# State-space rows kept by lag instead of by time step, and two groups of full-width matmuls cut into pieces of 32 stationary columns

## What is computed

```
u = h @ w_in                                # (256, 1024), 64 groups of 16 channels
per group, 64 complex states:
    bu = u_group @ bb^T                     # injection into the states
    h_t = a * h_(t-1) + bu_t                # scan over time
    y = Re(h @ c^T) + d * u                 # emission and skip
y = gelu(y); val, gate = split(y @ w_glu); out = val * sigmoid(gate)
```

## Time and profile before

| what | value |
|---|---|
| time, median of 3 runs | 767.78 us (765.35 to 768.37) |
| the profiled execution: its own time | 767.76 us |
| its span, first to last instruction | 765.8 us |
| TensorE busy (matmul records) | 727.7 us, 95% of the span |
| VectorE (DVE) | 530.4 us, 69% |
| ScalarE (ACT) | 411.9 us, 54% |
| GpSimd (POOL) | 127.7 us, 17% |
| mean granted TensorE clock | 0.984 |

### The profile page before, as it was taken

How to read it: one execution, slowest core, us unless ns; L and a number is a source line. 1 busy time by engine, 2 the same in 40 slices (tenths; PEclk the granted TensorE clock), 3 DMA queues, 4 the chain that set the end, 5 groups by cost and what they waited for, 6 DMA issues and landing times.

```text
span 765.8 us, 17216 instructions
## 1 busy us (share of the span) xinstructions
PE 727.7 (95%) x6636; PEld 660.5 (86%) x6636; DVE 530.4 (69%) x897; ACT 411.9 (54%) x682; POOL 127.7 (17%) x120
## 2 busy tenths in 40 slices
PE   4789999999999999999999999989999999999996
PEld 1478999457888999999999799979969999999995
DVE  4756665995488788777867686556567767676665
ACT  4244644565465556675567653325556555555554
POOL 1000000211015343434303254430000000000000
PEclk9799999999999999999999999989999999999998
DMA  8979755696755767667676041008725555555521
GB/s 315 378 272 383 255 190 165 255 406 246 283 215 182 280 187 257 209 238 238 221 260 204 3 138 58 29 29 342 263 73 192 177 183 174 192 191 165 192 83 56
DMA packets 46068, 156.61 MB, mean 205 GB/s; under 512 B 6016, under 2 KB 7312, under 8 KB 46016
## 3 DMA queue, kind: packets, MB, share of 16 engines
q1 hardware_dynamic: 43344, 148.26, 55.2%
q10 hardware_dynamic: 2160, 6.38, 2.2%
q0 software_dynamic: 512, 1.25, 0.4%
HBM read 154.82 MB, written 1.05 MB: 204 GB/s over the span
## 4 chain that ended last, share of the span: by engine, by line
PE 85%; DVE 7%; issue 3%; ACT 3%; POOL 1%; DMA 1%; DVEq 0%; POOLq 0%; ACTq 0%
PE up L368 13%; PE up L370 13%; PE up L369 13%; PE acc L368 9%; PE acc L369 9%; PE acc L370 9%; PE gv L410 5%; DVE wlo L1165 2%; PE misc L469 1%; PE up L752 1%; DVE tmp L1193 1%; PE up L765 1%; PE acc L740 1%; DMA ident<-in_ident 1%; PE acc L498 1%
## 5 line engine op out<-in xcount | busy, mean ns | idle before, releaser
L1165 DVE TENSOR_TENSOR wlo<-raw,whi 128x1024 fp32r<-128x1024 f32 x188 | 252.7, 1358 | 77.2 <-ACT whi L820 70.8
L368 PE MATMUL up<-hh,whi 128*128 128x256 f32 x896 | 255.7, 285 | 1.9 <-DVE hl L1198 1.9
L370 PE MATMUL up<-hh,wlo 128*128 128x256 f32 x896 | 253.5, 283 | 0.0
L369 PE MATMUL up<-hl,whi 128*128 128x256 f32 x896 | 253.5, 283 | 0.0
L820 ACT ACTIVATE whi<-raw 128x1024 fp32r<-128x1024 f32 x185 | 192.5, 1051 | 41.0 <-PE acc L370 26.3
L368 PEld LDWEIGHTS up<-hh,whi 128*128 128x128 f32 x896 | 171.7, 192 | 9.8 <-issue 3.8
L369 PEld LDWEIGHTS up<-hl,whi 128*128 128x128 f32 x896 | 171.8, 192 | 0.0
L370 PEld LDWEIGHTS up<-hh,wlo 128*128 128x128 f32 x896 | 171.8, 192 | 0.0
L1496 DVE SCALAR_TENSOR_TENSOR ffn<-up,conv,ffn 128x254 f32<-128x254 f32 (+1 forms) x176 | 72.7, 475 | 45.6 <-ACT ffn L1015 45.3
L368 PE MATMUL acc<-ah,whi 128*128 128x256 f32 x352 | 99.8, 284 | 0.6 <-DVE wlo L1165 0.6
L369 PE MATMUL acc<-al,whi 128*128 128x256 f32 x352 | 99.6, 283 | 0.0
(11 more groups left out here) (240 smaller groups left out, 920.6 us busy)
## 6 DMA issues: line engine op xcount, KB each, us to landing
raw<-in_w SPq DMA_DIRECT2D x188, 512.0 KB, 3.4
mraw<-in_mw SPq DMA_DIRECT2D x48, 512.0 KB, 6.1
arena<-in_mw SPq DMA_DIRECT2D x24, 512.0 KB, 9.7
raw<-in_w SPq DMA_DIRECT2D x12, 256.0 KB, 13.0
tmp<-in_mw SPq DMA_DIRECT2D x6, 512.0 KB, 7.7
ffn<-in_mw SPq DMA_DIRECT2D x6, 512.0 KB, 8.5
tmp<-in_mw ACTq DMA_DIRECT2D x4, 512.0 KB, 6.0
ffn<-in_mw ACTq DMA_DIRECT2D x4, 512.0 KB, 8.6
```

Of the source, the lines that this page charges most:

```text
L368: pe.matmul(out, w_h, xh, start=first, stop=False, skip_group_check=skip)
L369: pe.matmul(out, w_h, xl, start=False, stop=False, skip_group_check=skip)
L370: return pe.matmul(out, w_l, xh, start=False, stop=last, skip_group_check=skip)
L1165: dve.tensor_tensor(wlo[:, n % SPL, :], raw[:, n % RAW, :], whi[:, n % SPL, :].bitcast(F32), ALU.subtract).then_inc(lo_ready, 1)
```

## The change

It touches the state-space mixer and `spread_root`:

- `u` and `up` are kept with the lag outside: column l·64 + j instead of 4·j + l. The reads of `stack_u` and `lags` and the writes of `lags` and `emit` become contiguous. ACT's copy of the projection reads PSUM 4 columns apart, and ACT's gelu reads its input 64 columns apart to bring `yg` back into the order of time.
- `inject` and `spread_root` issue each matmul as four, of 32 stationary columns and 32 output partitions each, with the same moving columns.

```
-        u = ffn[:].rearrange("p (m j l) -> p m j l", m=KT, l=LCH)
+        u = ffn[:].rearrange("p (m l j) -> p m l j", m=KT, l=LCH)
...
                 for h in range(2):
-                    mm = pe.matmul(spread[:, h * P:(h + 1) * P], rt[:, h:h + 1].broadcast_to([P, P]), ident[:],
-                                   start=True, stop=True)
+                    for g in range(0, P, 32):
+                        mm = pe.matmul(spread[g:g + 32, h * P:(h + 1) * P], rt[:, h:h + 1].broadcast_to([P, 32]), ident[:],
+                                       start=True, stop=True)
...
-                                       ident[:, 32 * q:32 * q + 32], u[:, mt, :, l], start=True, stop=True)
+                                       ident[:, 32 * q:32 * q + 32], u[:, mt, l, :], start=True, stop=True)
...
-                        mm = pe.matmul(acc[:, 2 + mt % 2, (2 * q + r) * NJ:(2 * q + r + 1) * NJ],
-                                       bpow_r[:, r, c:c + P], ust[:, mt % 2, q, :], start=True, stop=True)
+                        for g in range(0, P, 32):
+                            mm = pe.matmul(acc[g:g + 32, 2 + mt % 2, (2 * q + r) * NJ:(2 * q + r + 1) * NJ],
+                                           bpow_r[:, r, c + g:c + g + 32], ust[:, mt % 2, q, :], start=True, stop=True)
...
-                y = up[:, mt % 2, 0:T].rearrange("p (j l) -> p j l", l=LCH)
+                y = up[:, mt % 2, 0:T].rearrange("p (l j) -> p l j", l=LCH)
                 for lag in range(LCH):
-                    pe.matmul(y[:, :, lag:LCH], kbd[:, mt, lag, :], u[:, mt, :, 0:LCH - lag],
+                    pe.matmul(y[:, lag:LCH, :], kbd[:, mt, lag, :], u[:, mt, 0:LCH - lag, :],
...
-                            mm = pe.matmul(y[32 * q:32 * q + 32, :, l], cpow[:, (l + 1) % 4, r, pair * 32:pair * 32 + 32],
+                            mm = pe.matmul(y[32 * q:32 * q + 32, l, :], cpow[:, (l + 1) % 4, r, pair * 32:pair * 32 + 32],
...
-                act.activation(yg[:, mt, :], yv[:, mt % 2, :], ACT.Gelu_apprx_tanh).then_inc(yg_ready, 1)
+                act.activation(yg[:, mt, :].rearrange("p (j l) -> p j l", l=LCH), yv[:, mt % 2, :].rearrange("p (l j) -> p j l", l=LCH),
+                               ACT.Gelu_apprx_tanh).then_inc(yg_ready, 1)
...
-                act.activation(ffn[:, m * T:(m + 1) * T], acc[:, m % 2, 0:T], ACT.Copy).then_inc(u_ready, 1)
+                act.activation(u[:, m, :, :], acc[:, m % 2, 0:T].rearrange("p (j l) -> p l j", l=LCH), ACT.Copy).then_inc(u_ready, 1)
```

## The result

| what | before | after |
|---|---|---|
| median of the compared runs | 766.64 us (764.66 to 768.37, 11 runs) | 762.22 us (761.55 to 765.09, 11 runs) |
| ratio | | 0.9949, interval 0.9935 to 0.9963 |
| profiled execution: own time, span | 767.76, 765.8 | 762.10, 760.1 |
| mean granted TensorE clock | 0.984 | 0.986 |

The ratio puts the change at the very edge of the 0.5% that counts. A second set of runs of the same kernel, 0.9962 (0.9949 to 0.9975), lies inside it. So: a gain of 0.4 to 0.5%, some 3 to 4 us.

What follows compares the result with a forecast made beforehand. TensorE was taken as the bound in the state-space stage's middle, at 8.90 us an iteration. Stage terms -4.09 + 0.75 + 0.6 + 1.1 = -1.64, with -0.35 for the root, gave -1.99 from 767.76: 765.8 us, range 762.3 to 768.3.

Steps and rivals of the forecast that it cites:

- The stack: TensorE's stack in the state-space stage: contiguous moving columns bring it to the emission's pace, -0.41 us each.
- The injection: TensorE's injection in the state-space stage: 64 pieces at the emission's pace plus switches of form, -0.51 us each.
- Lags and emission: TensorE's lags and emission groups in the state-space stage: no gain from the new column order.
- ACT: ACT's two copies in the state-space stage, now reading with a stride: no change from 0.383 us.
- Emission 0: First emission of the state-space stage: a DVE split goes ahead and delays POOL's chain, +0.75 us, between 0 and +1.1.
- The middle: Full stretch of the state-space iterations: one stall from DVE and POOL blocking each other, +0.6 us, between 0 and 1.9.
- Iteration 7: Last iteration of the state-space stage: five DVE operations meet POOL's last two, +1.1 us, between 0 and 1.5.
- The root: The root's spread at five norms: an earlier first weight load, together -0.35 us, between 0 and -0.8.
- (a): Rival for the whole kernel: TensorE alone decides, DVE and POOL blocks fall into slack, 763.3 us; chance 0.25.
- (b): Rival in the state-space stage: DVE and POOL become the bound, iterations settle at 8.36, total 767.1 us; chance 0.13.
- (c): Rival in the injection: pieces sharing moving columns don't overlap, +2.3 us on each, total 779 us; chance 0.06.
- (d): Rival in the emission: contiguous PSUM writing saves up to half of its 0.92 us, total 763.5 us; chance 0.04.

Runs made afterwards that it cites:

- a2_whole: The changed kernel run once more, unedited: ratio 0.9962 to the kernel before, state-space stage 73.97 us.
- e9_short_split: The changed kernel with DVE's weight splits of iterations 2 to 6 cut to 32 of 1024 columns: ratio 0.9958 to the kernel before, stage 71.17 us.
- e10_fill: The changed kernel with stack ahead of emission, skip 5 ahead of a split, and more GLU products ahead of emission 7: ratio 0.9899 to before, median 758.17 us.
- e12_gelu_plain: The changed kernel with the gelu reading and writing straight on, rows not returned to time order: stage 73.59 us, one execution of 763.50 us.
- e8_both: The changed kernel with the stack ahead of the emission and skip 5 ahead of a DVE split: ratio 0.9925 to the kernel before, median 760.82 us.
- e7_stack_first: The changed kernel with each tile's stack ahead of the emission of two tiles earlier: ratio 0.9939 to the kernel before, stage 73.43 us.

## Why the prediction came out as it did

The forecast was -1.99, and the ratio 0.9949 on its basis of 767.78 gives 763.9, -3.9; the second set's 0.9962 gives -2.9. The traces put the change's own part at 3.03 (2.37 in the first profile) plus 0.3. It moved in the forecast's direction, by twice the forecast, and landed between the forecast and "TensorE alone decides"; the median of the runs, 762.22, is 0.1 under the range's low end, with a basis 1.1 lower than the prediction's. On its own basis the time is inside the range. That is luck in part, since terms with opposite errors made it up: too little gross gain, too much for emission 0, too little for the middle. Step by step:

- **The stack:** forecast -0.41; the step from its first record to the next transposes is 3.53 for 4.02, -0.49. That the stride of the moving columns set its pace was right; the short last group gave more than I took.
- **The injection:** forecast -0.51; measured 0.71 less from its first record to the lags, 0.10 more ahead of it: -0.61. The 64 records took their 0.9, but I had charged the full price of a change of form at both ends (0.12 and 0.23 for a step that is anyway 0.11 long), and it is 0.10 ahead and 0.05 behind, the latter inside the lags. Together with the five stacks the gross gain was 5 x 0.49 + 4 x 0.61 = **4.89, not 4.09.** This is the largest term that was mis-sized, and the iteration without a wait was 7.79, not 7.98.
- **Lags and emission:** the emission's "nothing" was right (0.91 and 0.92). The lags' was 0.06 off, masked by the change of form (1.35 and 1.36).
- **ACT:** the copies read PSUM 4 columns apart at no price, 0.384 us. The gelu, of which the prediction gave no price, costs 0.25 more. It lay beside other work.
- **Emission 0:** forecast +0.75; measured 15.96 for 15.65, +0.3. The split went ahead of line 1777, as the step said, and POOL's chain took 5.61 instead of 4.86. But the chain had started 0.45 earlier, which the step left out. In the first profile the clock fell there as well (below), for another 1.0.
- **The middle:** forecast one stall, +0.6; measured two, 8.14 and 8.52 against 7.79, **+1.1.** The mechanism was right (POOL's last operation held by a split, 1.71). It didn't recur each time, so the case of 8.36 in every iteration stayed out.
- **Iteration 7:** forecast +1.1 of blocks; measured +0.7 up to lags 7, all of it blocks (2.83 for 2.12 in line 1609), and -0.2 behind, which is the clock and lay in the +-1.3 of the range. Lags 7 waited 5.00, as forecast.
- The sum with the measured terms is +0.3 - 4.89 + 1.1 + 0.7 - 0.2 = -3.0, and the stage has 3.03 (a2_whole). Forecast was -1.64: 0.8 from the gross gain, 0.5 from emission 0, 0.4 and 0.2 from the stage's end, less 0.5 from the middle.
- **The root:** forecast -0.35, measured about -0.3, beneath what the times can tell.
- **Rivals.** (a) is refuted by the waits in the middle, where the parts don't add (4.75 and 3.85), and by e9_short_split, though its total of -4.44 is no further off than the forecast's. (b) by iterations of 7.79. (c) by line 742 at the emission's pace. (d) by the emission's 0.91.

What stays open: what decides when the clock rises behind lags 7 (9.76 and 10.08 us to emission 7 in two profiles of the kernel before, 9.57 and 9.23 in two of the changed one), and so how much of the 0.2 there is the change's own.

## What to carry to other kernels

Find each wait that already stands ahead of the bounding engine and count only the tiles between two of them; then ask which pairs of DVE and POOL operations a shorter iteration makes meet, because the parts of a change can lose when joined what each gained alone. Move a wait only together with work that fills the place it moves to: here the skip moved ahead turned 5 us into 4 with a low clock, and e10_fill, which adds the stack's move and fills that place, is 1.0% faster than the kernel before. When one execution varies by 3 us ahead of the changed stage, measure from an instruction at the stage's head, and compare the granted clock of its parts before a difference is put down to an edit.

## What the runs showed of the hardware that I had not expected

- **ACT's strided read of SBUF cost time, its strided read of PSUM did not.** Reading 256 elements 64 columns (256 bytes) apart in SBUF took the gelu from 412 to 662 ns; reading 4 columns (16 bytes) apart in PSUM left the copy at 384:

```profile
L1111 ACT ACTIVATE ffn<-acc x8: 383/384/388, 429.8 to 483.8; 128x256 f32<-128x256 f32 x8
```

  The strides and the functions differ too, so whether memory or stride decides isn't settled; e12_gelu_plain shows that it isn't the gelu itself (409).
- **Writing PSUM 4 columns apart cost the emission nothing,** 0.92 us for 64 records against 0.91 when contiguous. The Trainium skill (PSUM — Partial Sum Buffer, Specifications) says that non-contiguous access slows matmuls significantly; for a matmul's output here the measurement says otherwise. Reading moving columns 16 bytes apart in SBUF is what cost: 26 ns a record in the stack before, and its group went from 1.11 to 0.63.
- **Four pieces of one weight block, with the same moving columns, are as fast as pieces with different ones:** 64 records in the time of the emission's (1.03 us up to the lags), faster than 16 whole ones at 0.11 each (1.74).
- **A wait of under 3 us can halve the clock.** Emission 0 waited 2.77 in the profile after, and the stretches there are:

```profile
443.20:445.90 2.70, 0.00 (x0) 0.00 (x0) 2.67 (x4) 0.00 (x0) 2.51 (x3) 0.83 0.70 215
445.90:447.60 1.70, 1.67 (x64) 1.70 (x68) 1.67 (x3) 0.00 (x0) 0.12 (x1) 0.50 0.05 12
```

  The emission ran at 1.2 GHz (group 1.94 in place of 1.10) and the iteration took 8.93. In a2_whole the same wait of 2.78 left the clock high and the iteration at 7.79. The same code takes 1.1 us more or not, by chance. It isn't the length of the wait: in e8_both 2.18 brought the clock down, in e7_stack_first and e10_fill 2.20 did not.
